# Attention values with V as the stationary operand, two heads on the column halves, and the reciprocals of the row sums transposed

## The reference

```python
q, k, v for branch a (top-k sparse attention) and branch b (window of 128 keys, with a sink logit)
p = softmax(logits)                        # 8 heads, 2 key/value heads, head size 64
o = einsum(p, v)                           # per head, 512 x 64
y_a = o_a @ w_branch_a ; y_b = o_b @ w_branch_b
mix = sigmoid(g_a) * y_a + sigmoid(g_b) * y_b
x = x + mix @ w_out
x = x + square(relu(rmsnorm(x) @ w_up)) @ w_down
return rmsnorm(x)
```

## Time and profile before

| | us |
|---|---|
| median of 3 runs (lowest, highest) | 1606.91 (1605.30, 1607.58) |
| profiled execution, its own time | 1606.37 |
| its span, first to last instruction | 1604.6 |
| mean granted TensorE clock | 0.998 |

### The profile page before, as it was taken

How to read it: one execution, slowest core, us unless ns; L and a number is a source line. 1 busy time by engine, 2 the same in 40 slices (tenths; PEclk the granted TensorE clock), 3 DMA queues, 4 the chain that set the end, 5 groups by cost and what they waited for, 6 DMA issues and landing times.

```text
span 1604.6 us, 19536 instructions
## 1 busy us (share of the span) xinstructions
PE 1587.7 (99%) x7590; PEld 1312.2 (82%) x7590; DVE 762.1 (47%) x1098; ACT 504.6 (31%) x745; POOL 709.1 (44%) x273
## 2 busy tenths in 40 slices
PE   8999999999999999999999999999999999999998
PEld 6887788888888988888888887877878988888886
DVE  6701588910156566666005389975563431023203
ACT  3012211210125444344214344246543442124312
POOL 4875189677761354454451003330133244344451
PEclk9999999999999999999999999999999999999999
DMA  5342032232333333333323222320034122223221
GB/s 199 103 132 79 1 109 82 82 127 80 105 106 105 95 89 105 98 85 105 105 84 108 81 79 79 105 74 6 28 103 134 42 91 105 105 79 105 105 93 65
DMA packets 123285, 147.00 MB, mean 92 GB/s; under 512 B 5143, under 2 KB 98375, under 8 KB 123208
## 3 DMA queue, kind: packets, MB, share of 16 engines
q1 hardware_dynamic: 121334, 141.05, 27.4%
q10 hardware_dynamic: 1874, 4.85, 0.9%
HBM read 143.79 MB, written 2.10 MB: 91 GB/s over the span
## 4 chain that ended last, share of the span: by engine, by line
PE 86%; DVE 8%; POOL 2%; issue 2%; ACT 1%; DMA 1%; DVEq 0%; SPq 0%; POOLq 0%; ACTq 0%
PE ps L631 26%; PE ps L633 25%; PE ps L632 25%; PE ps L773 3%; PE ps L1028 2%; DVE work L1800 2%; PE ps L850 2%; DVE top L1797 2%; POOL w_lo L584 1%; PE ps L1014 1%; PE ps L838 1%; DVE score L1785 1%; POOL w_hi L579 1%; PE ps L871 0%; DVE rope_u L1555 0%
## 5 line engine op out<-in xcount | busy, mean ns | idle before, releaser
L584 POOL TENSOR_TENSOR w_lo<-raw,w_hi 128x1024 fp32r<-128x1024 f32 x224 | 557.4, 2510 | 724.4 <-ACT w_hi L1072 721.7
L631 PE MATMUL ps<-hT_hi,w_hi 128*128 128x512 f32 (+1 forms) x928 | 356.4, 384 | 0.8 <-POOL w_lo L584 0.5
L632 PE MATMUL ps<-hT_lo,w_hi 128*128 128x512 f32 (+1 forms) x928 | 354.6, 382 | 0.0
L633 PE MATMUL ps<-hT_hi,w_lo 128*128 128x512 f32 (+1 forms) x928 | 354.6, 382 | 0.0
L1072 ACT ACTIVATE w_hi<-raw 128x2048 fp32r<-128x2048 f32 (+1 forms) x87 | 165.0, 1896 | 244.9 <-PE ps L631 210.5
L631 PEld LDWEIGHTS ps<-hT_hi,w_hi 128*128 128x128 f32 x928 | 174.8, 188 | 37.1 <-issue 2.3
L633 PEld LDWEIGHTS ps<-hT_hi,w_lo 128*128 128x128 f32 x928 | 174.6, 188 | 33.8
L632 PEld LDWEIGHTS ps<-hT_lo,w_hi 128*128 128x128 f32 x928 | 174.8, 188 | 33.2
L579 POOL TENSOR_TENSOR w_hi<-raw,cells 128x2048 fp32r<-128x2048 f32 x35 | 130.1, 3718 | 129.9 <-PE ps L631 128.3
L633 PE MATMUL ps<-w_hi,f_lo 128*128 128x512 f32 x400 | 155.6, 389 | 0.0
L631 PE MATMUL ps<-w_hi,f_hi 128*128 128x512 f32 x400 | 155.6, 389 | 0.0
(11 more groups left out here) (303 smaller groups left out, 2211.8 us busy)
## 6 DMA issues: line engine op xcount, KB each, us to landing
raw<-in_w_in SPq DMA_DIRECT2D x86, 512.0 KB, 4.6
raw<-in_w_up SPq DMA_DIRECT2D x76, 512.0 KB, 4.6
raw<-in_w_down SPq DMA_DIRECT2D x54, 512.0 KB, 4.2
raw<-in_w_out SPq DMA_DIRECT2D x16, 512.0 KB, 4.2
raw<-in_w_ret_o SPq DMA_DIRECT2D x8, 512.0 KB, 4.0
raw<-in_w_sgu_o SPq DMA_DIRECT2D x8, 512.0 KB, 4.1
x<-in_x SPq DMA_DIRECT2D x4, 512.0 KB, 6.0
raw<-in_w_branch_b SPq DMA_DIRECT2D x4, 512.0 KB, 4.3
```

The lines of the kernel that those rows point to most:

```text
L584: nc.gpsimd.tensor_tensor(lo[:, c], raw[:, s, c], hi[:, c].bitcast(f32), ALU.subtract).then_inc(unit_split, 1)
L631: first = nc.tensor.matmul(dst, a_hi, b_hi, start=start, stop=False)
L632: nc.tensor.matmul(dst, a_hi, b_lo, start=False, stop=False)
L633: return first, nc.tensor.matmul(dst, a_lo, b_hi, start=False, stop=stop)
```

## The change

The values are turned around: V (64 columns) is stationary and the transposed probabilities (128 columns) move. The two heads of a pair use key/value heads 0 and 1 and write partitions 0 to 63 and 64 to 127 of the same bank, so the result is features by tokens and is not transposed any more. The rows of the branch weights are loaded in the matching order of heads (`load_heads`).

The reciprocals must then stand along the tokens. A new event `sums` (p % 4 == 1) makes them on VectorE, each of the 8 sums repeated 64 times (`wide_ri`, 128x512); `out_T` (now p % 4 == 2) transposes `wide_ri`; ScalarE copies the result to `ri_T`, VectorE multiplies the values by it into `oTb`. For branch a an event `o_split` makes `oTa_hi` and `oTa_lo` from `oTb`.

Seven columns of `g_a` are computed ahead of attention and one in parts, in steps 2, 6, 10 and 14. In the first unit the transposes of the next tile stand after the first contraction step instead of the second, and two normalisations are done earlier in the orders of ScalarE and VectorE. The names of semaphores and buffers are left out below.

```diff
 HEAD = [0, 4, 1, 5, 2, 6, 3, 7]
-GA_IN = 6
+GA_IN = 7
 GA_PARTS = 4 * (KT - GA_IN)
-PARTS = [1 + 2 * n for n in range(GA_PARTS)] + [23 + n * 11 // 13 for n in range(13)] + [34, 34, 35]
+PARTS = [2 + 4 * n for n in range(GA_PARTS)] + [23 + n * 11 // 13 for n in range(13)] + [34, 34, 35]
...
                 step += [(kind, 2 * (p - back)), (kind, 2 * (p - back) + 1)]
-        if p > 4 and p % 4 == 3:
+        if p > 4 and p % 4 == 1:
+            step.append(("sums", p // 4 - 1))
+        if p > 4 and p % 4 == 2:
             step.append(("out_T", p // 4 - 1))
+        if p > 4 * NT + 4 and p % 4 == 3:
+            step.append(("o_split", p // 4 - 1))
...
         return part_of(n)[2] == part_of(n)[3] - 1
-    return kind != "values"
+    return kind not in ("values", "sums", "o_split")
...
 EVENTS = [e for step in ATTENTION for e in step]
-ACT_EVENTS = in_order(lambda e: 0 if e[0] == "probs_T" else 1)
+ACT_EVENTS = in_order(lambda e: 0 if e[0] in ("probs_T", "o_split") else 1)
...
         upto = at("upto", [P, S], B2 + 44 * KB)
-        o2 = at("o2", [P, 2, S], B2 + 48 * KB)
+        wide_ri = at("wide_ri", [P, 2, S], B2 + 48 * KB)
+        ri_T = at("ri_T", [P, S], B2 + 52 * KB)
...
                     sp.dma_start(part, of).then_inc(raw_loaded[u % 2] if u or per else first_loaded[h], 16)
+
+            def load_heads(u, src):
+
+                sp.wait_ge(unit_split, 2 * (u - 1))
+                dst = raw[:, u % 2, :].rearrange("p (k n) -> p k n", k=4)
+                for g in range(KV_HEADS):
+                    of = src[g * 4 * HD:(g + 1) * 4 * HD, :].rearrange("(k p) n -> p k n", p=HD)
+                    sp.dma_start(dst[g * HD:(g + 1) * HD, :, :], of).then_inc(raw_loaded[u % 2], 16)
...
                 for j in range(2):
-                    load(U0[phase] + j, rows(name)[:, :, j * 512:j * 512 + 512], 4)
+                    load_heads(U0[phase] + j, a[name][:, j * 512:j * 512 + 512])
...
                             first.then_inc(unit_started, 1)
-                        if tt < NT - 1 and kk == 1:
+                        if tt < NT - 1 and kk == 0:
...
                 unit_T(U0["g_a"] + j, T0["g_a"] + 2 * j, KT, 256, hT_hi, hT_lo)
+            column(U0["g_a"] + 3, G_A[6], KT, 256, 0, hT_hi, hT_lo)
...
                     t = event("out_T", s)
-                    pe.wait_ge(o2_made, s + 1)
-                    transposes(t, [o2[:, s % 2, n * P:(n + 1) * P] for n in range(4)])
+                    pe.wait_ge(ri_made, s + 1)
+                    transposes(t, [wide_ri[:, s % 2, n * P:(n + 1) * P] for n in range(4)])
+                    continue
+                if kind in ("sums", "o_split"):
...
                     transposes(event("probs_T", s), [probs[:, s % 4, n * P:(n + 1) * P] for n in range(nk)])
-                else:
+                elif s % 2 == 0:
...
                     elif s % HEADS == 0:
-                        pe.wait_ge(o2_made, turn - 1)
-                    await_evacuated(pe, event("probs_T", s))
+                        pe.wait_ge(o_made, turn - 1)
+                    for g in range(KV_HEADS):
+                        await_evacuated(pe, event("probs_T", s + g))
+                    col = slice(h % 4 * P, (h % 4 + 1) * P)
                     for n in range(nk):
-                        last = nc.tensor.matmul(ps[:, b, h * HD:(h + 1) * HD], probs_T[:, s % 4, n * P:(n + 1) * P],
-                                                value(k0 + n, h // 4), start=n == 0, stop=n == nk - 1)
-                    last.then_inc(values_made, 1)
-            for turn in range(NT, 2 * NT):
-                await_evacuated(pe, event("out_T", turn))
+                        for g in range(KV_HEADS):
+                            last = nc.tensor.matmul(ps[g * HD:(g + 1) * HD, b, col], value(k0 + n, g),
+                                                    probs_T[:, (s + g) % 4, n * P:(n + 1) * P],
+                                                    start=n == 0, stop=n == nk - 1)
+                            if n == nk - 1:
+                                last.then_inc(values_made[g], 1)
+            pe.wait_ge(oTa_made, NT)
...
-        FIRST_ACT = [("B", 0), ("B", 1), ("W", 0), ("W", 1), ("C", 0), ("B", 2), ("C", 1), ("B", 3), ("C", 2), ("C", 3)]
-        FIRST_DVE = [("B", 0), ("W", 0), ("C", 0), ("B", 1), ("C", 1), ("B", 2), ("C", 2), ("B", 3), ("C", 3)]
+        FIRST_ACT = [("B", 0), ("B", 1), ("W", 0), ("W", 1), ("C", 0), ("B", 2), ("B", 3), ("C", 1), ("C", 2), ("C", 3)]
+        FIRST_DVE = [("B", 0), ("W", 0), ("C", 0), ("B", 1), ("B", 2), ("C", 1), ("B", 3), ("C", 2), ("C", 3)]
...
                 evacuate(G_A[c], sig_a[:, c, :], ACT.Sigmoid)
-                if c % 2 and c < GA_IN - 1:
+                if c in (1, 3):
...
                     if s % HEADS == 0 and turn >= 2:
-                        act.wait_ge(o2_made, turn - 1)
+                        act.wait_ge(ri_made, turn - 1)
...
                     if k == 0:
-                        await_evacuated(act, event("out_T", NT - 1))
+                        act.wait_ge(o_made, NT)
...
                     if s >= 4:
-                        act.wait_ge(values_made, s - 3)
+                        act.wait_ge(values_made[1], s // 2 - 1)
...
                     t = event("out_T", s)
-                    view = bank(t).rearrange("p (k n) -> p k n", k=4)
+                    if s:
+                        act.wait_ge(o_made, s)
+                    evacuate(t, ri_T[:, :], ACT.Copy)
+                elif kind == "o_split":
                     tok = slice(TILE[s] * P, (TILE[s] + 1) * P)
-                    if s < NT:
-                        evacuate(t, oTb[:, :, tok], ACT.Copy, view)
-                    else:
-                        await_psum(act, t)
-                        hi_out.up(nc.scalar.activation(oTa_hi[:, :, tok], view, ACT.Copy))
+                    act.wait_ge(o_made, s + 1)
+                    hi_out.up(nc.scalar.activation(oTa_hi[:, :, tok], oTb[:, :, tok], ACT.Copy))
...
                     if s >= 4:
-                        dve.wait_ge(values_made, s - 3)
+                        dve.wait_ge(values_made[0], s // 2 - 1)
...
                     V.tensor_copy(probs_T[:, s % 4, 0:nk * P], ps[:, BANK[t], 0:nk * P]).then_inc(evacuated[BANK[t]], 1)
-                elif kind == "values" and s % HEADS == HEADS - 1:
-                    b = turn % 2
-                    if turn < NT:
-                        dve.wait_ge(sinks_exp, turn + 1)
-                        dve.wait_ge(probs_made, s + 1)
+                elif kind == "sums":
+                    b = s % 2
+                    dve.wait_ge(probs_made, HEADS * (s + 1))
+                    if s < NT:
+                        dve.wait_ge(sinks_exp, s + 1)
...
                         step.wait()
-                    dve.wait_ge(probs_made, s + 1)
-                    step.up(V.reciprocal(ri[:, b, :], rs[:, b, :]))
-                    if turn >= 2:
-                        await_psum(dve, event("out_T", turn - 2))
-                    dve.wait_ge(values_made, s + 1)
-                    step.wait()
-                    V.tensor_tensor(o2[:, b, :].rearrange("p (h d) -> p h d", h=HEADS),
-                                    ps[:, VALUES_BANK + b, :].rearrange("p (h d) -> p h d", h=HEADS),
-                                    ri[:, b, :, None].broadcast_to([P, HEADS, HD]), ALU.mult).then_inc(o2_made, 1)
-                elif kind == "out_T" and s >= NT:
+                    if s >= 2:
+                        await_psum(dve, event("out_T", s - 2))
+                    V.reciprocal(wide_ri[:, b, :].rearrange("p (j g d) -> p j g d", j=4, g=KV_HEADS),
+                                 rs[:, b, :].rearrange("p (g j) -> p j g", g=KV_HEADS)[:, :, :, None].broadcast_to(
+                                     [P, 4, KV_HEADS, HD])).then_inc(ri_made, 1)
+                elif kind == "out_T":
                     t = event("out_T", s)
+                    for g in range(KV_HEADS):
+                        dve.wait_ge(values_made[g], 4 * s + 4)
+                    await_evacuated(dve, t)
+                    V.tensor_tensor(oTb[:, :, TILE[s] * P:(TILE[s] + 1) * P],
+                                    ps[:, VALUES_BANK + s % 2, :].rearrange("p (k n) -> p k n", k=4),
+                                    ri_T[:, :].rearrange("p (k n) -> p k n", k=4), ALU.mult).then_inc(o_made, 1)
+                elif kind == "o_split":
+                    dst = (slice(None), slice(None), slice(TILE[s] * P, (TILE[s] + 1) * P))
                     hi_in.take()
-                    dst = (slice(None), slice(None), slice(TILE[s] * P, (TILE[s] + 1) * P))
-                    V.tensor_tensor(oTa_lo[dst], bank(t).rearrange("p (k n) -> p k n", k=4),
-                                    oTa_hi[dst].bitcast(f32), ALU.subtract).then_inc(evacuated[BANK[t]], 1)
+                    V.tensor_tensor(oTa_lo[dst], oTb[dst], oTa_hi[dst].bitcast(f32),
```

(8 more changed lines are left out.)

## The result

| | before | after |
|---|---|---|
| median, us | 1607.06 | 1613.03 |
| lowest to highest, executions | 1605.30 to 1607.58, 6 | 1611.38 to 1614.65, 6 |
| profiled execution, own time (span) | 1606.37 (1604.6) | 1612.14 (1610.3) |
| mean granted clock | 0.998 | 0.995 |

The ratio is 1.0038, with a 95% interval of 1.0026 to 1.0050: slower by 6.0 us. The forecast was 1608.2, its likeliest case 1605 to 1611, its whole range 1599 to 1619. Of its cases the one that came is the rival in which the clock falls in the pauses (1612.5).

What follows compares the result with a forecast made beforehand. TensorE, busy 99% of the span, was taken to bound the kernel. Terms -7.9 + 14.9 - 4.3 - 1.4 = +1.3 us gave 1607.7 on the profiled execution's scale, 1608.2 on the median's; likeliest 1605 to 1611, whole range 1599 to 1619.

Steps and rivals of the forecast that it cites:

- the rival in which the clock falls in the pauses: Attention stage: two or three falls of TensorE's granted clock in the new pauses, 1612.5 us, slower; chance 0.20.
- start: First unit: earlier transposes and rows remove TensorE's waits for `hT_lo` before three tiles, -1.4 us, at most 2.1.
- moved column: Seventh `g_a` column leaves the attention steps and runs ahead, partly in TensorE's 2.58 us of idle time: -4.3 us.
- values, halves in pairs: Attention value matmuls: two heads run together on the column halves, with a price for entering the split array: -7.9 us.
- pauses before `wide_ri`: Attention turns: TensorE waits for VectorE's wide reciprocal before transposing its result, +12.4 us in all.
- waits for a bank: After turns 3 and 4: next step's second logits wait for a bank VectorE frees late, 1.2 and 1.3 us more.
- clock: Attention pauses: the sum counted no falls of the granted clock, 0 us.
- the reciprocal: VectorE, once per attention turn: the 128x512 reciprocal takes 3.35 us, bounds 0.69 and 3.55 us.
- what the rival would have been: Attention values: column halves run one after the other, values +7.8 us, 1618 us in all, slower; chance 0.20.
- the forecast's lower bound: Moved `g_a` column: only the idle time ahead of attention is filled, -2.6 us.
- The split for free: Attention values and first unit: entering the split array costs near zero, start better packed, 1603 us; chance 0.12.
- the edits at nothing: Attention multiplications, ScalarE copies, `values_made` waits and reordered branch-weight loads: no cost; four more ScalarE copies, uncovered, 2.4 us.

Runs made afterwards that it cites:

- the start alone: Kernel before with only the first unit's edits (earlier transposes, two orders): 1605.55 us, ratio 0.9990.
- the column alone: Kernel before with seven instead of six `g_a` columns ahead of attention and one in parts, nothing else: 1602.05 us, ratio 0.9970.
- turned values, narrow: Kernel before with only the turned values, using an 8-sum reciprocal and a copy that repeats it: 1600.80 us, ratio 0.9962.
- the narrow form: Changed kernel with the reciprocal of 8 sums as before and a VectorE copy repeating it to 128x512: 1594.55 us, ratio 0.9925.
- work in the pauses: Changed kernel with filler identity matmuls on TensorE ahead of the wait for `wide_ri` in turns 0 to 4 and 7: 1608.84 us, ratio 1.0016.
- The serial run: Changed kernel with 8-sum reciprocal and copy, both heads of a pair on the same column half one after the other: 1606.28 us, ratio 0.9998.
- the order that shortens it: Changed kernel with 8-sum reciprocal and copy, VectorE multiplying by `ri_T` only after the next step's first logits: 1596.55 us, ratio 0.9941.
- the second measurement: Changed kernel with 8-sum reciprocal and copy, run again unchanged on another chip: 1595.57 us, ratio 0.9931.
- the wide form of the turned values: Kernel before with only the turned values and the 128x512 reciprocal, without first-unit and `g_a` column edits: 1615.72 us, ratio 1.0062.
- half of the wide reciprocal: Changed kernel with two of the four 128-column blocks of `wide_ri` made by the reciprocal, the others by copy: 1601.22 us, ratio 0.9967.

## Why the prediction was right or wrong

| term, us | forecast | measured | by |
|---|---|---|---|
| start | -1.4 | -1.3 | the start alone |
| moved column | -4.3 | -4.8 | the column alone |
| values, halves in pairs | -7.9 | -6.35 | turned values, narrow |
| pauses before `wide_ri` | +12.4 | +11.7 | rows of after |
| waits for a bank | +2.5 | +0.2 | rows of after, less those of the narrow form |
| clock | 0 | +6.7 (4.0 at least) | windows of after; work in the pauses |
| sum | +1.3 | +6.2, and 6.0 in the medians | |

**Right: what bounds the change and the reciprocal.** 3.35 us each, as extrapolated from 1, 8 and 16 elements to 512. The pauses by turn were forecast at 2.0, 2.2, 2.2, 1.8, 2.1, 0.1, 0.6 and 1.4; they are 1.8, 2.16, 2.16, 1.68, 1.99, 0, 0.4 and 1.43. Counting VectorE's own order, and the steps of TensorE that cover it, was enough for the pauses.

**Right: the halves pair.** Sixteen records take 1.02 us, against 8 x 0.115 + 0.19 = 1.11 forecast. The serial run shows what the rival would have been: 11.7 us more than the pairs, where the forecast had 15.7 for the values before the longer cover. The records account for 14.6 of that, and shorter logits take 2.9 back.

**Too large: the gain of the values.** In the narrow form the value records, each group from its start to the next instruction, take 19.9 us where those of before take 30.0: 10.1 less. But the transposes ahead of them take 0.56 or 0.59 us where four took 0.49, some 2.9 us over 32 steps: part of what entering the split array costs falls there. And the logits at the passage into turns 4 and 5, left open above, take 1.6 us more. That makes -10.1 + 2.9 + 1.6 = -5.6. The profiled execution of the turned values alone (1600.87) is 5.5 under that of before, but the two numbers agree in part by luck: that execution also has 1.7 us more of the low clock, and 1.0 us less from the first `y_a` matmul to the end (425.0 and 426.0 us), which makes -4.9 and leaves 0.6 unplaced. The medians differ by 6.35. The split was priced about right; the longer logits weren't in the sum.

**Wrong: the clock was left out of the sum.** This is the step that failed. The forecast knew the fall after the 2.58 us and its price of 1.7, put "two or three falls" into a rival with a chance of 0.20, and left the sum at zero because "each pause is shorter than that one, and work stands close on both sides". Neither kept the clock up: behind five pauses of 1.7 to 2.2 us there were four falls, 6.7 us by the windows, 5.4 to 6.4 by what the narrow form leaves over, and 4.0 at least by the fillers. Of the 4.9 us between the two sums the clock is 6.7 and the values 1.6; the bank waits give 2.3 back, the pauses 0.7, start and column 0.4 net. So the rival's 1612.5 is near the measured 1613.0 by luck, too: it had two or three falls for four, and the shortfall of the values and the surplus of the bank waits nearly cancel. The sum should also have counted the one fall of before as one that can go: neither the column alone nor the narrow form has it in its profiled execution. By those executions 1.7 of the column's gain is the clock's and 2.6 the moved work's, which is the forecast's lower bound, so that -4.3 came near -4.8 by a cause that it didn't name.

**Too large: the waits for a bank.** Of 1.2 and 1.3 after turns 3 and 4 only 0.47 is there, at 1136.59, and the narrow form has 0.34 of the kind elsewhere.

**A slip in a rival's sum.** The split for free was put at 1603. From 1608.2 its terms are -6 for the split, +2.5 for the shorter cover, and for the start 2 in place of the 1.4 already counted, -0.6: that is 1604.1. No conclusion hangs on it.

**Right: the edits at nothing.** The branch weights land in 6.2 us instead of 4.3, and no wait for them shows. The forecast overlooked the wait of VectorE for `ri_T` with logits behind it. Shortened by 9.5 us it gave no time back, though the order that shortens it adds 1.5 us of other waits, so that what it costs by itself isn't shown.

## What to carry to other kernels

Widen with a copy, not with an iterative operation: take the reciprocal of the few distinct values and repeat the result. This alone turns +6.0 us into -12.3 (-11.4 in the second measurement), and the version with it is the best here. When a change puts waits of about 2 us into an otherwise full TensorE, price the clock with them, from the fall that the trace already holds: here it came to between a third (4.0 of 11.7 us) and more than half (6.7) of what the waits cost. And a part that seems independent, like the moved column, may be the cover of another's latency: what each is worth depends on the other.

## What the hardware showed

- A reciprocal on VectorE costs some 0.16 us and 6.25 ns for each element of a row, from 1 to 512 elements (162, 200, 253 ns and 3.35 us for 1, 8, 16 and 512), where copies and multiplications of 128x512 take 0.49 and 0.69 us. The Trainium skill, VectorE: DVE Perf Modes, section First, the fixed hardware budget, gives it a repeat count of 8, from which 4.3 us had been estimated. The measurement is 3.35, and it decides.
- Two f32 matmuls of 64 stationary columns on the two column halves run fully side by side: the records of a pair start 7 ns apart in the trace, and a pair takes 0.11 us, as one record did. The Trainium skill, TensorEngine Tiling, section Tiling Modes, says that different tiles can multiply in parallel, and the trace agrees.
- The length of a pause doesn't by itself decide on the clock. In after the window behind the 2.16 us at 1104.74 reads 1.00 while that behind the 2.16 us at 1091.74 reads 0.86, and in the wide form of the turned values 1.67 us pass without a fall, while in after a fall follows 1.68. With half of the wide reciprocal a fall follows 1.01 us of idle time at the start of the stage, in the narrow form none follows the 1.02 there. What else decides isn't settled.
